# Loads of x, gated rows and queries in two parts of 120 + 8, 104 + 24 and 88 + 40 partitions, in a one-core hybrid decoder layer with expert retrieval

## The reference

```
h  = x + W_out[concat(RMSNorm(Attn(q,k,v)), Conv(c))],  [q|k|v|c] = RMSNorm(x) W_in
def chunk(xc):                                  # 128 tokens
    experts = ...top-k of product keys...       # (128, 8, 16)
    u_sel = u_tab[experts]
    act = gelu(einsum('chkd,cd->chk', u_sel, xc))
    w = gates * act
    v_sel = v_tab[experts]
    return einsum('chk,chkd->cd', w, v_sel)     # y;  out = h + y
```

## Time and profile before

| | |
|---|---|
| median of 3 runs | 2847.38 us (2847.22 to 2849.18) |
| the profiled execution | 2849.06 us, of which the span is 2847.2 us |
| TensorE / VectorE / GpSimd busy | 78% / 76% / 69% of the span |
| mean rate of the DMA engines over the span | 395 GB/s |

### The profile page before, as it was taken

The page is one execution under the profiler, slowest core; times in us unless marked ns, Lnnn a source line. Parts: engine busy times, 40 slices in busy tenths (PEclk is TensorE's granted clock), DMA queues, the critical chain, the costliest instruction groups (busy, mean ns, idle before and its releaser), DMA issues.

```text
span 2847.2 us, 30140 instructions
## 1 busy us (share of the span) xinstructions
PE 2232.5 (78%) x7669; PEld 760.9 (27%) x7669; DVE 2154.0 (76%) x5486; ACT 822.4 (29%) x1998; POOL 1978.4 (69%) x2086
## 2 busy tenths in 40 slices
PE   8999978778667776788768886787868787666667
PEld 4644433223212231232312331132312322111111
DVE  5889979568887788778887788788888858755452
ACT  3223422331124221352115421263115611111111
POOL 1446656777777777777777777777777777777775
PEclk9999989989868896789868897699868997666667
DMA  7269999999999999999999999999999999999998
GB/s 252 86 268 412 392 391 361 419 418 419 419 419 417 416 419 418 406 406 419 419 417 409 395 419 419 416 403 418 419 419 402 415 419 419 414 419 420 415 418 353
DMA packets 322020, 1124.75 MB, mean 395 GB/s; under 512 B 36097, under 2 KB 43289, under 8 KB 321848
## 3 DMA queue, kind: packets, MB, share of 16 engines
q0 software_dynamic: 294912, 1073.87, 93.1%
q1 hardware_dynamic: 26920, 48.94, 4.8%
q10 hardware_dynamic: 16, 0.00, 0.0%
HBM read 1114.30 MB, written 8.39 MB: 394 GB/s over the span
## 4 chain that ended last, share of the span: by engine, by line
DMA 38%; issue 20%; POOL 13%; PE 11%; DVE 6%; ACT 2%; POOLq 0%; ACTq 0%; DVEq 0%
DMA w_kept<-in_peer_u,experts 15%; DMA ring_v<-in_peer_v,v_experts 10%; DMA ring_v<-in_peer_v,gate_rows 8%; POOL w_kept L1818 7%; PE psum L1923 6%; POOL ring_v L1818 6%; DMA w_kept<-in_peer_v,gate_rows 2%; DVE w_kept L2261 2%; DMA w_kept<-in_peer_v,v_experts 1%; PE psum L560 1%; PE psum L1849 1%; DVE log_keep L2184 1%; PE psum L1304 1%; DVE acc L2217 1%; DMA qT_spill<-qT_out 1%
## 5 line engine op out<-in xcount | busy, mean ns | idle before, releaser
L1923 PE MATMUL psum<-ring_v,diag 128*64 128x512 f32 x3224 | 1134.6, 788 | 482.6 <-DMA ring_v<-in_peer_v,v_experts 226.4
L2261 DVE CUSTOM_DVE_ANT_0 w_kept<-w_kept,psum 128x1024 f32<-128x1024 f32 x896 | 1087.9, 1218 | 491.8 <-DMA w_kept<-in_peer_u,experts 486.7
L1818 POOL DMA_INDIRECT w_kept<-in_peer_u,experts x896 | 847.7, 946 | 282.2 <-issue 226.6
L2084 ACT ACTIVATE diag<-stacked,weights 128x64 f32<-128x64 f32 x992 | 303.0, 339 | 790.7 <-PE psum L1923 577.6
L1923 PEld LDWEIGHTS psum<-ring_v,diag 128*64 128x64 f32 x3224 | 211.4, 161 | 1175.4 <-issue 672.9
L1818 POOL DMA_INDIRECT ring_v<-in_peer_v,v_experts x430 | 406.5, 945 | 147.7 <-issue 112.1
L1818 POOL DMA_INDIRECT ring_v<-in_peer_v,gate_rows x376 | 357.4, 950 | 157.3 <-issue 96.9
L1923 PE MATMUL psum<-w_kept,diag 128*64 128x512 f32 x744 | 242.0, 736 | 92.3 <-DMA w_kept<-in_peer_v,gate_rows 40.1
L560 PE MATMUL psum<-w_sb,xnT 128*128 128x512 f32 x640 | 285.7, 602 | 0.3 <-ACT xnT L809 0.3
L2217 DVE SCALAR_TENSOR_TENSOR acc<-conv_in,taps,acc 128x128 f32<-128x128 f32 x720 | 204.8, 346 | 0.5
L504 POOL DMA_INDIRECT w_kept<-in_peer_u,experts x128 | 120.3, 940 | 83.9 <-issue 30.8
(11 more groups left out here) (279 smaller groups left out, 2009.2 us busy)
## 6 DMA issues: line engine op xcount, KB each, us to landing
w_kept<-in_peer_u,experts POOLq DMA_INDIRECT x1024, 13.0
w_sb<-in_w_in SPq DMA_DIRECT2D x4, 2048.0 KB, 17.0
ring_v<-in_peer_v,v_experts POOLq DMA_INDIRECT x430, 13.1
ring_v<-in_peer_v,gate_rows POOLq DMA_INDIRECT x376, 13.0
x_in<-in_x SPq DMA_DIRECT2D x8, 512.0 KB, 9.2
w_kept<-in_w_out SPq DMA_DIRECT2D x1, 4096.0 KB, 14.8
h_res<-in_x SPq DMA_DIRECT2D x8, 512.0 KB, 6.5
w_kept<-in_peer_wq SPq DMA_DIRECT2D x2, 2048.0 KB, 8.6
```

What stands on the lines that cost most here:

```text
L1818: nc.gpsimd.indirect_dma_start(slot(kind, n), None, peer_u[0] if kind == "u" else peer_v[0], bass.IndirectOffsetOnAxis(index[:, e:e + 1], ...
L1923: last = nc.tensor.matmul(y_ps[d * GROUP:(d + 1) * GROUP, j * BANK:(j + 1) * BANK], diag[:, e % DIAGS, :], slot("v", n)[:, d * BANK:(d + 1 ...
L2084: nc.scalar.activation(diag[:, e % DIAGS, :], S.stacked[:, :], ACT.Copy, scale=weights[:, e:e + 1]).then_inc(diagonal, step_of(c, e))
L2261: nc.vector.tensor_tensor_reduce(out=row, in0=row, in1=hn, scale=1.0, scalar=0.0, op0=ALU.mult, op1=ALU.add, accum_out=dots[:, e:e + 1]).t ...
```

## The change

Each of the three loads of `load_front` is issued as two DMAs over a part of the partitions each, and the three waits count the additional increments. The tuples at the top are the parts: x in 120 and 8 partitions, the gated rows (C) in 104 and 24, the queries (Q) in 88 and 40. The loads of phase 0 into the same tiles stay single DMAs. No other instruction changes.

```diff
+X_PARTS, C_PARTS, Q_PARTS = ((0, 120), (120, P)), ((0, 104), (104, P)), ((0, 88), (88, P))
...
-        dve.wait_ge(S.x_in, 16 * (f + 1))
+        dve.wait_ge(S.x_in, 16 * (1 + len(X_PARTS) * f))
...
                 if f > 1:
                     sp.wait_ge(S.z_ready, UNITS * f)
-                    sp.dma_start(qT[:, :, :].rearrange("p b t -> p (b t)"),
-                                 qT_spill[f]).then_inc(S.q_in, 16)
+                    for lo, hi in Q_PARTS:
+                        sp.dma_start(qT[lo:hi, :, :].rearrange("p b t -> p (b t)"),
+                                     qT_spill[f, lo:hi, :]).then_inc(S.q_in, 16)
                 if f > 2:
                     sp.wait_ge(S.tapped, TAP_OPS * f)
-                    sp.dma_start(conv_in[:, :, :], hT_spill[:, :, f * P:f * P + HALO + P]).then_inc(S.c_in, 16)
+                    for lo, hi in C_PARTS:
+                        sp.dma_start(conv_in[lo:hi, :, :],
+                                     hT_spill[lo:hi, :, f * P:f * P + HALO + P]).then_inc(S.c_in, 16)
                 sp.wait_ge(h_added, 2 * f)
-                sp.dma_start(S.h_res[:, :], x[0, f * P:(f + 1) * P, :]).then_inc(S.x_in, 16)
+                for lo, hi in X_PARTS:
+                    sp.dma_start(S.h_res[lo:hi, :], x[0, f * P + lo:f * P + hi, :]).then_inc(S.x_in, 16)
...
-                pe.wait_ge(S.q_in, 16 * f)
+                pe.wait_ge(S.q_in, 16 * (1 + len(Q_PARTS) * (f - 1)))
...
-                dve.wait_ge(S.c_in, 16 * (f - 1))
+                dve.wait_ge(S.c_in, 16 * (1 + len(C_PARTS) * (f - 2)))
```

## The result

The changed kernel takes 2873.6 us (2871.5 to 2876.3, 4 runs) against 2848.3 us for the kernel before beside it: 25.3 us more, a ratio of 1.0088 with a 95% interval of 1.0077 to 1.0100. The forecast was 13 us less.

A forecast was written before the change was run, and what follows sets the result against it. The prediction took the slowest DMA engine's total work as the bound: 7.5 (x) + 3.1 (queries) + 3.8 (gated rows) = 14.4 us saved, of which 13 arrive, so 2847.4 - 13 = 2834.4 us; range 2829 to 2850.

The forecast's parts named there:

- the laggard's total work is the time of the row phase: Row phase, 540 to 2830 us: ring buffers wait for the slowest DMA engine's part of each gather; account 2259 of 2290 us.
- The second slowest engine is next to bound: Limit on the gain in the row phase: the other engines' room below the slowest, between 11 and 40 us.
- The 7 us of the end: End of the span: one engine works alone about 7 us late, counted as the least room of the others.
- the rival of the pile: Second parts go whole to one engine, 34.6 us more there: 2871 to 2882 us; chance 0.07, shared with a new wait.
- the 3.5 of the second parts: Loads after 540 us: an engine that gets all second parts carries 0.9 + 1.6 + 1.0 = 3.5 us more.
- If an engine keeps its 8 rows in the first part, the first part leaves out one, three and five engines: The three loads: second parts go to 8, 12 and 10 engines; one engine, left out of all three, saves 14.4 us.
- the engine left out is the one that lags: Row phase: the slowest engine is the one relieved of all three loads, 13 us faster, 2834 us; chance 0.62.
- the rival of 2850.9: Slowest engine keeps its 8 rows and gets second parts, up to 3.5 us more; chance 0.25 with all no-relief cases.
- The bytes are the same. What can change is which engine carries them.: The three loads: only the dealing of bytes to engines changes, each engine's share of a gather counted at 1.244 us.
- a sum of 0: The change's gain by the skill page's rule that two transfers to disjoint partitions aren't worth it: none.
- The signs to look for: Right: one or two gathers more in each of six windows, shallower boundary dips; wrong: unchanged counts, equally deep dips.
- Waits: SyncE's 18 more DMAs cost nothing: 7.6 us to spare for gated rows, 229 for queries of chunk 3.

## Why the prediction was wrong, point by point

*"the laggard's total work is the time of the row phase"*: borne out, but for the slower gathers' packets in two of the traces that nothing here explains. Even work of 12.5 us on every engine cost 10.3; 22 us on the first 4, 8 or 12 engines cost 21 to 22; 22 us on the first two cost 3.

*"The second slowest engine is next to bound", room of 11 to 40 us*: the first two engines have about 19 us (22 less 3.2, of which the interval leaves 0 to 5); of the others no run tells. The 7 us of the end, which I took for a sure part of it, are not: in the kernel split by columns one engine is alone for 2 to 3 us only. And where the rival of the pile names the room, 7 to 36 us is the room less the 3.5 of the second parts, not the room.

*"If an engine keeps its 8 rows in the first part, the first part leaves out one, three and five engines"*: right, by the 124 closing packets.

*"the engine left out is the one that lags"*: wrong, and named there as the weakest step. The laggard is the third or fourth engine in the dealing. If the second parts are dealt in the same order, it keeps its 8 rows and gets a share of each of them. I gave the engine left out more than two to one on the thought that an uneven load sits at an end. The Trainium skill (DMA: Bandwidth & Descriptors, Latency and other measured facts) says that engines 7 and 15 are usually the slower ones. That doesn't hold here, if engines are dealt from the lowest number, as the Trainium skill says on the same page (why a DMA increments its semaphore by 16): it is engine 2 or 3. This step alone would have made the result at most +3.5, the rival of 2850.9.

*"The bytes are the same. What can change is which engine carries them."*: the step that made the sign wrong by far. It leaves out which partitions an engine writes, and with it takes the time of a packet as fixed (1.244 us for each engine's share of a gather, whatever runs beside it). Parts of 112 and 16, with even bytes, cost 13.6 us, and 64 and 64 cost 21.0; both at a DMA share of 1.03 with 386 and 375 instead of 416 GB/s. With the change it is 373. Of the 25.3 us the imbalance has at most the 3.5 of my term; the rest is the engines' slower packets, 24.5 us for the mean engine in the trace (of an execution that took 27.2 us more), 18.2 of them the gathers'. The Trainium skill's rule against such splits (DMA: Bandwidth & Descriptors, rules for kernel authors), which I had quoted with a sum of 0, pointed the right way, but it names no loss: its reason is that both transfers use the same engines anyway. The split by columns shows that two DMAs are as good as one.

*The rival "slower" (pile on one engine, 2871 to 2882)*: the time came out there, by luck; the mechanism didn't. A part that goes to one engine would close with one packet, and the count rules that out.

*The signs to look for*: I had looked for one or two gathers more in each of the six windows, or unchanged counts if I was wrong. That they could become fewer (18 in all) was not among the signs.

*Waits*: right. For chunk 3 the gated rows landed 11.3 us after their issue, not the 10.6 of the median, so 6.9 us were to spare. SyncE's longer issues (1.84 us for the gated rows) and later landings brought no wait. The first tap of chunk 3 in the changed kernel (start 640.2, no idle time before it):

```profile
L2219 DVE TENSOR_SCALAR acc<-conv_in,taps,vec x4: 342/343/344, 640.2 to 640.9; 128x128 f32<-128x128 f32 x4
```

That the slowdown is at the *ports* of SBUF is inferred, not seen. The traces don't record which engine writes which partition; in the runs that lose, engine and partition change together, and no run changed the port and kept the engine. By the Trainium skill (DMA: Bandwidth & Descriptors, the descriptor swizzle) an engine's 8 rows of a 128-partition transfer are two groups of 4, 32 partitions apart, which share a port, one port to an engine; a run of 7 or 8 neighbours is not such a set. What the laggard's extra work consists of also stays open. An estimate from the packet records of the kernel before fits the fetches of instructions: the 64 packets of queue 8 took 63 us together, and 2650 + 136 + 63 = 2849 us is the whole span of 2847.2 for an engine that carried them all. But no record names its engine.

## What to carry to other kernels

When the DMA engines are full, let a plain load cover all 128 partitions: here every cut by partitions slowed the gathers beside it, and the packets of x themselves. If a load must be cut, cut it by columns, which cost next to nothing here. Before work is moved off the slowest engine, find out which one it is: a few HBM-to-HBM DMAs in 2, 4 or 8 pieces that don't join loaded just the first engines here, and the set with the one that lags answered with nearly its full price. Read rate and share together: the same share at a lower rate means slower packets, not idle engines.

## What I had not expected of the hardware

- One or two of the 16 DMA engines seem to set this kernel's time, and they are neither the first two in the dealing nor the last: 22 us more on two engines cost 3, on four 21.
- 6.7 MB of plain loads in other cuts, 0.6% of the 1125 MB, cost 14 to 25 us, because the gathers beside them slow down too. The bytes, the data packets and, with 112 + 16 and 64 + 64, the number of engines are the same.
- A DMA from HBM to HBM with adjoining rows was cut over all 16 engines though its first dimension was 8; with gaps it stayed on 8.
- On one chip the medians of all kernels were 3259 to 3266 us at 343 to 345 GB/s, and differences of 14 and 21 us vanished there.
